# Delta rule: the masked blocks of the inverse's levels on the vector engine, GpSimd with the scaled rows alone

## What is computed

```python
def gdn_chunked(q, k, v, g, beta, s0):
    ...
    diff = gcum[..., :, None] - gcum[..., None, :]
    decay = jnp.exp(jnp.where(tri_incl, diff, -jnp.inf))
    kb = kc * bc[..., None]
    vb = vc * bc[..., None]
    a_mat = jnp.where(tri_strict, jnp.einsum('nbhid,nbhjd->nbhij', kb, kc) * decay, 0.0)
    eye = jnp.eye(cs, dtype=jnp.float32)
    t_mat = lax.linalg.triangular_solve(eye + a_mat, jnp.broadcast_to(eye, a_mat.shape),
                                        left_side=True, lower=True, unit_diagonal=True)
    u = jnp.einsum('nbhij,nbhjd->nbhid', t_mat, vb)
    ...
    kdec = kc * jnp.exp(gcum[..., -1:] - gcum)[..., None]
    def step(s, xs):
        ...
        v_new = u_i - jnp.einsum('bhck,bhkv->bhcv', w_i, s)
        o_i = jnp.einsum('bhck,bhkv->bhcv', qg_i, s) + jnp.einsum('bhij,bhjv->bhiv', at_i, v_new)
        s = s * ge_i[..., None, None] + jnp.einsum('bhck,bhcv->bhkv', kd_i, v_new)
        return s, o_i
```

## Time and profile before

| | us |
|---|---|
| median of 3 timed runs | 3057.45 |
| lowest and highest of them | 3050.35, 3060.89 |
| the profiled execution | 3059.8 |
| span of the profiled execution, first to last instruction | 3058.0 |
| mean granted TensorE clock over the span | 0.962 |
| the delta rule's four tiles, in the span | about 1848 to 2062 |

### The profile page before, as it was taken

One profiled execution on the slowest core, in us unless ns is written; L12 is line 12 of the kernel. 1 busy time (PEld: TensorE's weight loads), 2 busy tenths in 40 slices (PEclk: granted clock), 3 DMA queues, 4 the chain that ended last, 5 costly groups with the idle time before them and its releaser, 6 DMA issues. The chain is left out here.

```text
span 3058.0 us, 69550 instructions
## 1 busy us (share of the span) xinstructions
PE 2823.3 (92%) x31424; PEld 2084.1 (68%) x31424; DVE 574.2 (19%) x1400; ACT 368.0 (12%) x911; POOL 74.7 (2%) x96
## 2 busy tenths in 40 slices
PE   5889999999999999999999997779999999888999
PEld 2577866669999989999987446674444444445883
DVE  0121001121001001001012214443222211232331
ACT  0111001111000000000002112221111100122210
POOL 0000000000000000000000002210000000000000
PEclk9899999999999999999998898889999999979999
DMA  8883443348999999999981110001122211311442
GB/s 341 321 344 131 154 155 131 117 166 331 381 380 379 391 371 387 384 379 381 395 360 38 46 69 15 2 2 55 69 75 76 83 67 72 110 42 55 152 151 83
DMA packets 80413, 584.32 MB, mean 191 GB/s; under 512 B 8912, under 2 KB 8912, under 8 KB 10064
## 3 DMA queue, kind: packets, MB, share of 16 engines
q1 hardware_dynamic: 79920, 580.15, 49.2%
q10 hardware_dynamic: 288, 1.05, 0.1%
HBM read 580.11 MB, written 1.05 MB: 190 GB/s over the span
## 5 line engine op out<-in xcount | busy, mean ns | idle before, releaser
L1419 PE MATMUL ps<-arena,ring 128*64 128x88 f32 x14336 | 555.2, 240 | 26.3 <-issue 23.0
L1419 PEld LDWEIGHTS ps<-arena,ring 128*64 128x64 f32 x14336 | 549.1, 137 | 31.5 <-issue 29.3
L2655 PE MATMUL ps<-hT,ring 128*128 128x256 f32 (+2 forms) x1472 | 456.8, 473 | 5.6 <-ACT hT L471 3.4
L2655 PEld LDWEIGHTS ps<-hT,ring 128*128 128x128 f32 x1472 | 276.1, 192 | 185.2 <-issue 166.3
L358 PE MATMUL ps<-ring,arena 128*128 128x512 f32 x896 | 390.2, 596 | 4.7 <-DVE arena L2561 3.6
L358 PEld LDWEIGHTS ps<-ring,arena 128*128 128x128 f32 x896 | 170.9, 191 | 217.5 <-issue 211.9
L1511 PE MATMUL ps<-arena,ring 128*64 128x88 f32 x7168 | 279.0, 239 | 16.9 <-issue 16.8
L1511 PEld LDWEIGHTS ps<-arena,ring 128*64 128x64 f32 x7168 | 273.8, 137 | 26.1 <-issue 26.1
L930 PE MATMUL ps<-hT,ring 128*128 128x256 f32 (+1 forms) x736 | 152.7, 370 | 2.6 <-ACT hT L469 2.6
L1528 ACT ACTIVATE arena<-ps 128x88 f32<-128x88 f32 x224 | 54.5, 243 | 827.7 <-PE ps L1419 827.7
L1549 DVE TENSOR_TENSOR arena<-arena,ps 128x88 f32<-128x88 f32 x224 | 55.1, 246 | 520.9 <-ACT arena L1528 520.9
(11 more groups left out here) (459 smaller groups left out, 2199.3 us busy)
## 6 DMA issues: line engine op xcount, KB each, us to landing
ring<-in_stream SPq DMA_DIRECT2D x547, 1024.0 KB, 7.0
par<-in_params SPq DMA_DIRECT2D x1, 3397.0 KB, 28.6
h<-in_x ACTq DMA_DIRECT2D x2, 512.0 KB, 8.0
cx<-in_ctx SPq DMA_DIRECT2D x2, 512.0 KB, 29.5
out<-h SPq DMA_DIRECT2D x4, 256.0 KB, 2.0
par<-in_params SPq DMA_DIRECT2D x1, 941.0 KB, 6.1
```

Of the source, the lines that this page charges most:

```text
L1419: last = nc.tensor.matmul(ps[m:m + 64, up_bank[j], half * P:half * P + CAP], w[:, k, half * P + m:half * P + m + 64], hTe[:, k, :], start= ...
L2655: last = nc.tensor.matmul(ps[:, 2 * BANKS_CONV[f % RING] + half, tok], w[:, k, half * P:half * P + P], hT[:, k, tok], start=(k == 0), stop ...
```

## The change

The two multiplications by a mask move from GpSimd to VectorE. `X` of level 1 stands on VectorE directly behind `TM`. `X` of the next level stands on VectorE behind a wait for the level's first product. GpSimd keeps the two rows; its wait `after_all` now stands ahead of them. GpSimd's count is taken out of the lane's `chain` until the rows are adopted at the end of the levels, so inside the levels only the additions to `r_` (L2439) wait for GpSimd.

```diff
+                @block.vector
+                def _(dve):
+                    dve_done.by(nc.vector.tensor_tensor(compact(X), compact(Atc), level(1), ALU.mult))
+
                 @block.gpsimd
                 def _(pool):
                     after_all(pool)
-                    pool_done.by(nc.gpsimd.tensor_tensor(compact(X), compact(Atc), level(1), ALU.mult))
-                x_known = pool_done.n
-
-                @block.gpsimd
-                def _(pool):
                     nc.gpsimd.tensor_tensor(heads(r_), heads(vt[:, T, :]), vecs(be), ALU.mult)
                     pool_done.by(nc.gpsimd.tensor_tensor(heads(kdec), heads(kt[:, T, :]), vecs(ed), ALU.mult))
                 rows_known = pool_done.n
-                chain[-1][pool_done] = x_known
+                chain[-1].pop(pool_done, None)
                 yield
...
                     if lev < 5:
-                        @block.gpsimd
-                        def _(pool):
-                            pool.wait_ge(pe_done.sem, p1_known)
-                            nc_x = nc.gpsimd.tensor_tensor(compact(X), compact(Atc), level(lev + 1), ALU.mult)
-                            x_next = pool_done.by(nc_x)
+                        @block.vector
+                        def _(dve):
+                            dve.wait_ge(pe_done.sem, p1_known)
+                            dve_done.by(nc.vector.tensor_tensor(compact(X), compact(Atc), level(lev + 1), ALU.mult))
```

## The result

| | before | after |
|---|---|---|
| median, us | 3060.89 (7 runs) | 3038.28 (7 runs) |
| lowest and highest | 3050.35, 3068.93 | 3035.19, 3041.01 |
| ratio, with its 95% interval | | 0.9933 (0.9916 to 0.9949) |
| profiled execution, span | 3058.0 | 3033.4 |

The change makes the kernel 0.67% faster, about 20 us (22.6 between the two medians), where 6.7 were forecast. The time lies outside the range given, and the gain is three times the sum.

A forecast was written before the change was run, and what follows sets the result against it. TensorE, 92% busy, was taken to stand still in the delta rule's chains of short instructions; 3.3 + 1.6 + 1.8 = 6.7 us off the median 3057.45 gave 3050.8, range 3042.5 to 3060.

The forecast's parts named there:

- The clock rival (c): Delta rule tiles: full clock returns before L2387 in three tiles, 3.9 us more, 10.6 saved, 3046.8 us; chance 0.25.
- Entry: Lane's start, TM to TensorE's first product: 0.88 us instead of 1.54, 0.65 saved five times, 3.3 us.
- Queue: First tile, lane 0's mask behind lane 1's mask and rows on GpSimd: 2.67 us becomes 1.05, 1.6 saved once.
- Rounds: Both lanes in their levels: lane 1's second products leave earlier, rounds 3.5 us instead of 3.7, 1.8 us in four tiles.
- Cover: VectorE work queued behind the new masks' waits, lane 0's L2424 and lane 1's L2330: both costed at nothing.
- signs of being wrong: New instructions at 1 us or more beside rows, rounds still 3.7, later L2424, or tile clock outside 0.84 to 0.87.
- (a): Rounds: the mask becomes the wait again, on VectorE; rounds give nothing, 4.9 us saved, 3052.6 us; chance 0.12.
- (b): First tile: GpSimd's rows hold VectorE, the queue's 1.6 stays lost, 5.1 us saved, 3052.4 us; chance 0.08.
- the paragraph on the rule: SBUF contention: lane 1's second-level mask held until GpSimd's rows finish, about 2 us; sum unchanged if rows follow lane 0's mask.
- (d): Rounds: clock stays down in two rounds per tile, costing 16.8 us, slower by 10, 3067.5 us; chance 0.05.

The follow-up runs named there:

- The part alone: Kernel before with only the level 1 mask moved to VectorE, levels 2 to 5 left on GpSimd: ratio 0.9974, delta rule 225.5 us against 229.2.
- the late wait: Kernel before, all masks on GpSimd, second products no longer waiting for the next level's mask: ratio 0.9963, delta rule 223.1 us.
- the kernel with the levels alone: Kernel before with only the masks of levels 2 to 5 moved to VectorE, level 1 left on GpSimd: ratio 0.9952, delta rule 223.4 us.
- 14 clears: Kernel before plus 14 tiny VectorE clears as a pause at the start of the latent attention: ratio 1.0001, latent attention 173.4 us.

## Why the prediction was wrong

**The step that failed** is the last sentence of the part on what bounds the kernel: "TensorE's order is the program's, so all that follows the stage moves with it." It moves, but it doesn't keep its length. The latent attention, 570 us later and with no changed line, takes 173.4, 171.7, 166.4 or 163.0 us by where it comes to lie. The clock rival (c) was the right mechanism at the wrong place: it looked for the clock only in the four tiles, and so its 10.6 us were held for the most that the clock could bring. Of the 21.8 us behind the first stretch, 10.4 are the latent attention, and 2.5 the two other unchanged stretches, each of which has one low stretch of the clock less in the changed kernel. The range, 3042.5 to 3060, was made from the delta rule alone.

**The sum itself**, point by point:

1. *Entry.* 0.88 us from TM to the product, measured 0.90. The part alone gave 3.7 us where its steps gave 3.6; as said above, the second agreement is in part luck.
2. *Queue.* 1.05 us from lane 1's first product to lane 0's second, measured 0.88. Here the step was right, its reason only half: it was put down to the queue of GpSimd, and the late wait shows that the queue may stay if the products don't wait for it.
3. *Rounds.* 3.5 us forecast, 3.54 measured. From lane 1's TM to the application of the inverse in lane 0 the four tiles got shorter by 2.46, 1.69, 1.49 and 0.86, together 6.5, where the steps give 6.0 (2.7 in the first tile and 1.1 in each other). The first and the last fall short and the middle two go beyond, so that the sum comes so near is in part luck too.
4. *Cover.* The two costs put at nothing were nothing. Lane 0's subtractions begin no later behind their products than before. The only late ones are lane 1's of the fourth level, 0.38 us behind their products instead of 0.14, held by lane 0's last subtractions as the prediction said.
5. *What was mis-sized* is the sum of 6.7 against 8.9. From lane 0's TM to lane 1's TM in the first tile the steps gave 0.65, measured were 1.96 (13.24 to 11.28). Two rows show the reason, the kernel before and the changed one, 4 to 5 us behind lane 0's TM:

```profile
1854.00:1855.00 1.00, 1.00 (x7) 0.50 0.00 0
```

```profile
1851.00:1852.00 1.00, 1.00 (x12) 1.00 0.00 0
```

The clock has come back already in the changed kernel. Another 1.6 us fell away at the end of lane 1's last tile, and 1.3 were lost at lane 1's third entry. These are the clock too, both ways: the kernel before has a stretch at 0.50 from 2057.96 to 2061.38, in that last tile, which the changed kernel lacks, and at the third entry the changed kernel has one of 6.8 us where the kernel before has 3.4. All three net of each other are 1.6 (1.3 and 1.6, less 1.3); the half microsecond of point 3 is most of the rest of the missing 2.2.

Two of the prediction's own signs of being wrong came: a new instruction of over 1 us beside the rows, and a granted clock outside 0.84 to 0.87 in the tiles. The first two tiles, each from 1.5 us ahead of lane 0's TM to the same point of the next, had 0.86 and 0.87 before and now have (TensorE alone):

```profile
1845.50:1890.30 44.80, 35.74 (x640) 0.89 0.01 2
1890.30:1942.90 52.60, 40.64 (x680) 0.90 0.01 2
```

**The rivals.** (a), the mask as the new wait, didn't happen: L2381 of lane 1 and L2411 of lane 0 leave one behind the other. (b), the rows that hold VectorE, did happen, though not to lane 0's mask of the third level, for which (b) had its price, but to lane 1's of the second, which the paragraph on the rule had named; there it cost nothing. The table by line and shape of the changed kernel shows how often (line, engine, operation, names, shapes, count | busy us, mean ns | idle time ahead and what ended it):

```profile
L2403 DVE TENSOR_TENSOR hT<-par 128x256 f32<-128x256 f32 x16 | 10.2, 638 | 11.5 <-PE ps L2381 11.5
L2403 DVE TENSOR_TENSOR arena<-hT,par 128x256 f32<-128x256 f32 x16 | 7.5, 471 | 0.0
```

At 0.43 us each the 16 of lane 1 would be 6.8 us; they are 10.2, four of them longer by 0.85, one in each tile, and one of lane 0's. The Trainium skill's rule (SBUF — State Buffer, "Who interferes with whom") said that a VectorE instruction with two SBUF operands is blocked by a GpSimd instruction that reads SBUF and was first. The trace agrees, with 1.27 us for 0.42. The instruction ends 0.27 us after the row in progress. In the kernel with the levels alone it meets the same row 0.35 us after its start, ends 0.29 after it and takes less:

```profile
1858.76 1.04 POOL L2371 TENSOR_TENSOR hT<-arena 128x512 f32<-128x512 f32 x1
1859.11 0.97 DVE L2404 TENSOR_TENSOR hT<-par 128x256 f32<-128x256 f32 x1 [1.95 <-PE ps L2382]
```

So the hold lasts as long as the row. The held mask met the second of the two rows each time, never the first, so whether it would wait for both is not shown. (c) is told above; as it was priced, with the clock back ahead of L2387 in three tiles, it did not come, as L2381 to L2411 take 3.05 us there in the changed kernel too. (d) didn't happen in the rounds.

The chances were honest about the sign and not about the size: 0.25 for faster by over 0.3%, which is what came, and not by the way that (c) describes.

## What to carry to other kernels

Before an instruction is moved to a faster engine, look at whether the one that waits for it reads it at all: in the levels the wait was the cost, and moving the wait bought about as much as moving the work. Where TensorE's clock moves between its two levels, a change of a few microseconds shifts everything behind it against these moves, so look in the profile of before for places where long matmuls follow an idle gap of a microsecond or two, and count a gain or a loss there among the cases, however far away it is. Compare kernels by stretches between the same instructions; the median alone would have given this change more than twice its own worth. And trace more than one execution where the granted clocks of the timed runs fall into two groups.

## What the runs showed of the hardware that was not expected

**The clock can stay down under full load.** The kernel before, TensorE alone, at the latent lanes:

```profile
2706.50:2716.50 10.00, 10.00 (x11) 0.50 0.00 0
2716.50:2726.90 10.40, 8.59 (x23) 0.50 0.00 0
```

For 10 us TensorE has no gap in its rows and the clock remains at 0.50; in the changed kernel the same matmuls run at 1.00. The Trainium skill (TensorE: Matmul & The Clock Gate, Part 1) says that the idle state is the throttled one and that activity releases it. Here activity in the sense of the timeline did not release it. Why not is open; no run took it apart, and what the runs show is only that with work in the idle time ahead the clock didn't fall, and that the same idle time in the changed kernel brought no fall.

**The same few lengths come back.** 173.4 us came in three traces (the kernel before twice, and with 14 clears), 163.0 in three others and 171.7 in two, each within 0.1 us, though the delta rules ahead of them differ. A pause of 1.74 us vanished in one of them, made good by 3.4 us less at 0.50 right behind it.

**A tiny clear** of 128x4 on VectorE, each waited for by the next, takes 0.12 us, where 0.22 had been read off the rotation's instructions.
